# Moving the key products, the decay and a 64x64 block inverse of a chunked gated delta rule beside the input projection

## What is computed

```
gc = cumsum(gdec); decay = where(i >= j, exp(gc_i - gc_j), 0)
A  = I + strict_lower((k*beta) @ k.T * decay);  T = inverse(A)
u = T @ (v*beta);  w = T @ (k*beta*exp(gc));  qk = (q @ k.T) * decay
v_new = u - w @ S;  o = (q @ S)*exp(g) + qk @ v_new
S = S*exp(g_last) + k_dec.T @ v_new            # the only chain from chunk to chunk
```

## Time and profile before

| what | value |
|---|---|
| median of 3 runs | 2875.92 us (2875.68 to 2878.38) |
| profiled execution | 2880.71 us, its span 2878.8 us |
| TensorE busy | 2641.6 us, 92% of the span |
| VectorE, ScalarE, GpSimd busy | 1296.5, 712.8, 444.4 us |
| mean granted clock of TensorE | 0.958 of full speed |
| HBM traffic | 144.32 MB read, 49.27 MB written |

### The profile page before, as it was taken

One profiled execution on the slowest core, in us unless ns is written; L12 is line 12 of the kernel. 1 busy time (PEld: TensorE's weight loads), 2 busy tenths in 40 slices (PEclk: granted clock), 3 DMA queues, 4 the chain that ended last, 5 costly groups with the idle time before them and its releaser, 6 DMA issues.

```text
span 2878.8 us, 39434 instructions
## 1 busy us (share of the span) xinstructions
PE 2641.6 (92%) x14704; PEld 2379.2 (83%) x14704; DVE 1296.5 (45%) x2190; ACT 712.8 (25%) x1269; POOL 444.4 (15%) x1039
## 2 busy tenths in 40 slices
PE   5999999974799999766999999999789999999997
PEld 4999999954788888635889899898678888888886
DVE  5444400003655555354444544445454444444445
ACT  5232211113233333104122121221422121222212
POOL 4000000004566665111000000000420000000002
PEclk9999999986899999877999999999889999999999
DMA  4122222124334333215111011111221111111111
GB/s 139 54 75 78 66 82 71 59 72 129 87 92 118 109 96 88 63 29 172 45 44 58 29 58 44 44 58 31 80 81 45 44 44 44 44 44 44 44 36 66
DMA packets 200686, 194.74 MB, mean 68 GB/s; under 512 B 27147, under 2 KB 172235, under 8 KB 197514
## 3 DMA queue, kind: packets, MB, share of 16 engines
q1 hardware_dynamic: 200594, 193.53, 22.2%
HBM read 144.32 MB, written 49.27 MB: 67 GB/s over the span
## 4 chain that ended last, share of the span: by engine, by line
PE 50%; POOL 2%; issue 1%; ACT 0%; DMA 0%; DVE 0%; SPq 0%; DVEq 0%; POOLq 0%; ACTq 0%
PE bank L124 17%; PE bank L126 17%; PE bank L125 17%; ACT f_relu L142 0%; DMA f_up_raw<-in_w_up_dram 0%; POOL f_acc L1586 0%; PE bank L179 0%; POOL f_acc L1584 0%; POOL fn_rs L113 0%; POOL fn_ms L147 0%; POOL ff_rs L113 0%; POOL ff_rt L111 0%; POOL ff_rt L110 0%; POOL fn_rt L111 0%; POOL fn_rt L110 0%
## 5 line engine op out<-in xcount | busy, mean ns | idle before, releaser
L124 PE MATMUL bank<-f_h_hi,f_up_lo 128*128 128x344 f32 (+1 forms) x1536 | 493.9, 322 | 4.5 <-DVE f_up_lo L1688 2.4
L1693 DVE TENSOR_TENSOR f_acc<-bank,f_acc 128x512 f32<-128x512 f32 x512 | 353.2, 691 | 320.5 <-PE bank L126 320.1
L126 PE MATMUL bank<-f_h_hi,f_up_hi 128*128 128x344 f32 (+1 forms) x1536 | 492.3, 321 | 0.0
L125 PE MATMUL bank<-f_h_lo,f_up_hi 128*128 128x344 f32 (+1 forms) x1536 | 492.1, 320 | 0.0
L124 PE MATMUL bank<-f_dn_hi,f_z_lo 128*128 128x512 f32 x1088 | 432.8, 398 | 0.5 <-ACT f_relu L1621 0.5
L126 PE MATMUL bank<-f_dn_hi,f_z_hi 128*128 128x512 f32 x1088 | 429.6, 395 | 0.0
L125 PE MATMUL bank<-f_dn_lo,f_z_hi 128*128 128x512 f32 x1088 | 428.4, 394 | 0.0
L124 PE MATMUL bank<-h_hi,w_lo 128*128 128x412 f32 (+3 forms) x1000 | 351.7, 352 | 2.1 <-DVE w_lo L427 2.1
L125 PE MATMUL bank<-h_lo,w_hi 128*128 128x412 f32 (+3 forms) x1000 | 351.1, 351 | 0.0
L126 PE MATMUL bank<-h_hi,w_hi 128*128 128x412 f32 (+3 forms) x1000 | 350.9, 351 | 0.0
L124 PEld LDWEIGHTS bank<-f_h_hi,f_up_lo 128*128 128x128 f32 x1536 | 290.9, 189 | 7.9 <-DVE f_up_lo L1688 2.7
(11 more groups left out here) (342 smaller groups left out, 3229.0 us busy)
## 6 DMA issues: line engine op xcount, KB each, us to landing
f_up_raw<-in_w_up_dram SPq DMA_DIRECT2D x64, 512.0 KB, 4.8
f_dn_raw<-in_w_down_dram SPq DMA_DIRECT2D x64, 512.0 KB, 3.7
p_dram<-y SPq DMA_DIRECT2D x24, 1024.0 KB, 4.6
w_raw<-in_w_in_dram SPq DMA_DIRECT2D x24, 512.0 KB, 5.8
xres<-in_x_prompt_dram SPq DMA_DIRECT2D x16, 512.0 KB, 4.6
x_dram<-x SPq DMA_DIRECT2D x16, 512.0 KB, 3.0
f_acc<-x_dram SPq DMA_DIRECT2D x16, 512.0 KB, 5.0
out_y_prompt_dram<-f_acc SPq DMA_DIRECT2D x16, 512.0 KB, 2.7
```

The lines of the kernel that those rows point to most:

```text
L124: pe.matmul(out, wl, xh, start=start and k == 0, stop=False, skip_group_check=skip)
L125: pe.matmul(out, wh, xl, start=False, stop=False, skip_group_check=skip)
L126: last = pe.matmul(out, wh, xh, start=False, stop=stop and k == n - 1, skip_group_check=skip)
L1693: dve.tensor_tensor(dst, bank, dst, ALU.add).then_inc(s["y_added"], 1)
```

## The change

- **Projection.** The 8 columns of a and b are the first tile, not the last; the tiles are reordered (keys first, then queries, values, gMLP v, gate, u), and the loops are unrolled. `gates` runs beside tiles 1 to 3. A new class `Keys` makes, for every chunk, the key product k k^T (one `by_head` on TensorE), the decay (`decay` on GpSimd, `exp` on ScalarE) and on VectorE the norm of the keys and the scaled matrix N, stored in `n_dram`; one chunk per tile at tiles 6 to 12, two at tiles 13 to 16, the last at tile 17. At tile 17 the 64x64 diagonal blocks of all chunks and heads (2 x 4 x 16 = 128 of them, one on each partition) are loaded back in 8 DMAs with runs of 256 bytes, VectorE inverts them by elimination during tiles 18 to 24 (62 steps of two dependent operations on up to 961 elements per partition), and the inverses are stored in `t_dram` at the end of the stage.
- **Mixer.** Key product, decay of N, GpSimd's 16x16 inversion, its DRAM round trip, the masks and two of the three doubling levels are gone. The level from 64 to 128 is left (`x_ready`, `y_ready`), and moved into the pass that loads the chunk. There are 18 passes with three stages (f = n, q = n - 1, o = n - 2). The sums of squares are made by ScalarE with `accum_out`, one for each head, in place of products with ones and a reduction; one `dve_rsqrt` per pass serves both norms. w_o's product is cut in 4 parts. `oT_hi`, `oT_lo`, `xres` and `x1` have two buffers. `build_u` makes the turned inverse in 6 small transposes.

```
+TILES = [None] + [*range(4, 8), *range(0, 4), *range(8, 12), *range(20, 24), *range(12, 16), *range(16, 20)]
+KEYS_AT = {**{6 + n: [n] for n in range(7)}, **{13 + n: [7 + 2 * n, 8 + 2 * n] for n in range(4)}, 17: [15]}
...
+    def load_blocks(self, sp):
+        sp.wait_ge(self.s["n_stored0"], 8 * NCH)
+        sp.wait_ge(self.s["n_stored1"], 8 * NCH)
+        for b in range(2):
+            for h in range(H):
...
+                sp.dma_start(self.blk[rows, :, :], src).then_inc(self.s["blk_loaded"], 16)
...
+    def scale(self, dve, n):
...
+        dve.tensor_tensor(heads(nm), heads(bank[:, :]), across(c.ident[:]), ALU.mult).then_inc(s["diag_made"], 1)
...
+        dve.tensor_reduce(self.ss[:], heads(nm), AX.X, ALU.add).then_inc(s["ss_made"], 1)
...
+        dve_rsqrt(dve, s["rsqrt"], n * DVE_RSQRT_STEPS, rk, self.ms[:], self.rt[:])
...
+        for h in range(H):
+            ins = dve.scalar_tensor_tensor(out=head(nm, h), in0=head(bank, h), scalar=c.negb[:, n, h:h + 1],
+                                           in1=head(self.em[n % 2], h), op0=ALU.mult, op1=ALU.mult)
...
+    def eliminate(self, dve, j):
...
+        rows, cols = HALF - 1 - j, j
+        col = blk[:, j + 1:HALF, j:j + 1].to_broadcast([P, rows, cols])
+        row = blk[:, j:j + 1, 0:j].to_broadcast([P, rows, cols])
...
+        self.own.did(dve, dve.tensor_tensor(part, col, row, ALU.mult))
+        self.own.did(dve, dve.tensor_tensor(below, below, part, ALU.add))
```

```
+            dve.wait_ge(s["vb_squared"], f + 1)
+            dve.tensor_scalar(ms[:, H:H + 1], ss8[:], 1.0 / HW, EPS, ALU.mult, ALU.add).then_inc(s["ms_made"], 1)
...
+            dve_rsqrt(dve, s["rsqrt"], n * DVE_RSQRT_STEPS, rs[:], ms[:], rt[:])
...
+            dve.tensor_tensor(heads(oa[:]), heads(bO), along(rs[:, 0:H]), ALU.mult).then_inc(s["oa_part"], 1)
...
+            dve.scalar_tensor_tensor(out=vbn[:], in0=bF, scalar=rs[:, H:H + 1], in1=c.v_gain[:],
+                                     op0=ALU.mult, op1=ALU.mult).then_inc(s["vbn_made"], 1)
...
+            dve.tensor_tensor(heads(av[:]), heads(vt[:]), along(c.alpha[:, f, :]), ALU.mult).then_inc(s["av_made"], 1)
...
+            dve.tensor_scalar(epsq[f % 2][:], ssq[:], EPS, DK * EPS, ALU.add, ALU.mult).then_inc(s["epsq_made"], 1)
...
+            dve.tensor_tensor(oT_lo[q % 2][:, H:KT, :], heads(ob[:]), oT_hi[q % 2][:, H:KT, :].bitcast(F32),
+                              ALU.subtract).then_inc(s["oTb_lo"], 1)
...
+            dve.tensor_tensor(qkm[:], bE, emQ[:], ALU.mult).then_inc(s["qkm_made"], 1)
```

and in ScalarE's order, after `o_ready`, come the four squares of the output, then, after `pt_k`, the four scaled copies `kd`, then the square of `vb`, the four squares of q and the copy `xs`:

```
+            for h in range(H):
+                ins = act.activation(head(sqo, h), head(bO, h), ACT.Square, accum_out=oss[:, h:h + 1])
...
+            act.activation(junk[:], bF, ACT.Square, accum_out=ss8[:]).then_inc(s["vb_squared"], 1)
...
+                ins = act.activation(head(junk_q, h), head(bD, h), ACT.Square, accum_out=ssq[:, h:h + 1])
...
+            act.activation(xs[:], bY[0:HALF, 0:H * HALF], ACT.Copy).then_inc(s["xs_made"], 1)
```

More of the change, by code:

```diff
@@ L551, in softplus_gates, with kind_of, steps_at, gates @@
     return act, dve, g_made
-def gates(c, io, st):
-    nc, sem, psum = c.nc, c.sem, c.psum
+NB5 = 5
+WB = 412
+HALF = P // 2
+NEVER = 1000.0
+TILES = [None] + [*range(4, 8), *range(0, 4), *range(8, 12), *range(20, 24), *range(12, 16), *range(16, 20)]
+NT = len(TILES)
+KEYS_AT = {**{6 + n: [n] for n in range(7)}, **{13 + n: [7 + 2 * n, 8 + 2 * n] for n in range(4)}, 17: [15]}
+LAST_KEYS = 17
+def kind_of(t):
+    f = TILES[t]
+    return "ab" if f is None else "conv" if f < NCONV else "gate" if f < NCONV + H else "plain"
+def steps_at():
+    total = sum((HALF - 1 - j) * j for j in range(1, HALF - 1))
+    tiles = range(LAST_KEYS + 1, NT)
+    out, done, j = {t: [] for t in tiles}, 0, 1
+    for n, t in enumerate(tiles):
+        while j < HALF - 1 and (done < total * (n + 1) / len(tiles) or t == NT - 1):
+            out[t].append(j)
+            done += (HALF - 1 - j) * j
+            j += 1
+    return out
+STEPS_AT = steps_at()
+def gates(c, io, st, bank, const_made):
+    nc, sem = c.nc, c.sem
     al = st.sb("al_b", [P, H])
@@ new lines, in pe @@
+    def pe(eng, step):
+        if step == 1:
+            for t in range(NCH):
+                last = eng.transpose(bank[0][:, t * 8:(t + 1) * 8], c.ab[:, t * P:(t + 1) * P], c.ident[0:8, 0:8])
+            last.then_inc(ab_turned, 1)
+        elif step == 2:
+            eng.wait_ge(g_made, 1)
+            eng.wait_ge(const_made, CONST_MADE)
+            eng.matmul(bank[1][:, 0:NCH * H], c.upto[:], flat, start=True, stop=True).then_inc(sums, 1)
+            eng.matmul(bank[1][:, NCH * H:2 * NCH * H], c.ones[:], flat, start=True, stop=True).then_inc(sums, 1)
+        else:
+            eng.wait_ge(sums_copied, 1)
+            eng.transpose(bank[0][0:NCH * H, P:2 * P], flat, c.ident[:]).then_inc(g_turned, 1)
@@ new lines, in mix @@
+    ssq, ss8, oss = sb("mx_ssq", [P, H]), sb("mx_ss8", [P, 1]), sb("mx_oss", [P, H])
+    ms, rt, rs = (sb("mx_" + n, [P, H + 1]) for n in ("ms", "rt", "rs"))
+    epsq = two("mx_epsq", (P, H))
+    xres, x1 = two("xres", (P, D)), two("x1", (P, D))
+    wo_raw = (x1[1][:], xres[1][:])
+    oT_hi, oT_lo = two("oT_hi", (P, KT, P), F32R), two("oT_lo", (P, KT, P), F32R)
+    S, ga = c.S, c.ga
+    names = """kt_loaded qt_loaded v_loaded gate_loaded vb_loaded ut_loaded gb_loaded t64_loaded n21_loaded xres_loaded0 xres_loaded1
+        x1_stored0 x1_stored1 delta_stored         zeroed
+        pt_v pt_g pt_b pt_q pt_k qk_ready x_ready y_ready p_ready gm_ready w_ready o_ready sd_ready oT_ready wo_ready
+        x1_made oTa_lo oTb_lo ob_sum u_turned u_final r_made ms_made rsqrt epsq_made vbn_made av_made
+        qkm_made oa_part s_updated
+        xs_made oTa_hi oTb_hi eg_made v_copied g_copied q_squared vb_squared kd_made e_made w_made o_squared
+        oa_made dif_made sel_made ob_made qe_made gg_made""".split()
@@ new lines, in x1_add, with build_u @@
+        wait(dve, s[f"x1_stored{o % 2}"], 16 * (o // 2))
+        dve.tensor_tensor(x1[o % 2][:, cols], (bG, bH)[half], xres[o % 2][:, cols], ALU.add).then_inc(s["x1_made"], 1)
+    def build_u(dve, f):
+        t = heads(T64[f % 2][:])
+        u = heads(U[:])
+        q32 = HALF // 2
+        for b in range(2):
+            for a in range(2):
+                at = b * HALF + a * q32
+                dve.transpose(u[at:at + q32, :, at:at + q32], t[at:at + q32, :, a * q32:(a + 1) * q32])
+            low, up = b * HALF + q32, b * HALF
+            ins = dve.transpose(u[up:up + q32, :, low:low + q32], t[low:low + q32, :, 0:q32])
+        ins.then_inc(s["u_turned"], 1)
@@ L1091, in sp_pass @@
-        if i is not None:
-            sp.wait_ge(s["n_stored"], 16 * (i + 1))
-            wait(sp, s["tb_made"], i)
-            for h in range(H):
-                diagonal = io["n_dram"][i].rearrange("(b r) -> b r", b=BD)[:, 0:SB * HW]
-                blocks = diagonal.rearrange("b (i f) -> b i f", f=HW)[:, :, h * P:h * P + SB]
-                sp.dma_start(blkN[h * BD:(h + 1) * BD, :, :], blocks).then_inc(s["blk_loaded"], 16)
-        if f is not None and f + 1 < NCH:
-            load_raw(sp, f + 1)
@@ L1114, in sp_pass @@
+        if n + 1 < NCH:
+            load_raw(sp, n + 1)
         if n < 2:
```

1133 lines of the change are left out of this document (524 added, 609 removed).

## The result

The changed kernel takes 2797.36 us (median of 4 runs, 2787.67 to 2799.49) where the kernel before takes 2875.8 us: a ratio of 0.9725, 95% interval 0.9696 to 0.9754. That is 78 us less. Run again later beside two of the experiments it took 2797.29 us (ratio 0.9732, 0.9715 to 0.9749). The prediction said 2780, 96 us less, with a range of 2745 to 2815: the direction and the range were right, the gain was 17 us too large.

A forecast was written before the change was run, and what follows sets the result against it. Steady mixer passes were taken as bound by TensorE's work plus its wait for oTb_lo: mixer 30 us later, pass 2 at 718.5, 14 passes of 25.9, sample stage at 1118.8 not 1214.7; 96 less, 2780 us, range 2745 to 2815.

The forecast's parts named there:

- the chain: Mixer's steady pass: pt_b, square, root, then VectorE operations to oTb_lo, which TensorE awaits; a pass of 25.9 us.
- GpSimd's hold: End of a mixer pass: GpSimd's oa and dif slow VectorE's av and oTb_lo, adding 1.4 us.
- The elimination: Projection, tiles 18 to 24: VectorE's inversion of the diagonal blocks takes 111 us, at 0.16 us + 1.04 ns an element.
- the fourth rival: Projection: strided operand makes elimination elements cost 2.3 ns or more, 216 us or more in all; 2875 to 2900, chance 0.04.
- exposed stores: Projection's end: last y and the inverses, 3 MB, go out with nothing to hide them; 12 us against 1.3.
- TensorE's own pass: Mixer's steady pass: TensorE's work sums to 21.8 us, 22.3 corrected, if nothing waits.
- The half clock: Mixer: a 2.8 us stall halves TensorE's clock about half the time, 1.8 us each; 0.9 a pass taken.
- the blocks are there 20 to 27 us into tile 18: Projection: block load of 8 to 14.6 us plus 2 to land makes TensorE wait once, before tile 20; 1.5 us taken.
- The third rival: Projection: block load and elimination 25 to 40% dearer, plus a longer stall at tile 20; 2792 to 2815, chance 0.10.
- the forecast with 0.58: Main case: mixer passes of 24.9 to 26.9 us, total 2766 to 2794, chance 0.58.
- The mixer's first turn: Mixer's start: chunk 0's loads delay the constants, so the first pass begins 15.2 us in, at 674.8.
- the ring of two: Mixer's start: w_o's pieces come through two buffers, holding pass 2 back to 718.5 us.

The follow-up runs named there:

- e3: Changed kernel with VectorE making oTb_lo right after the first of the two sums, not at the end of the pass: 2732.69 us, ratio 0.9489.
- e12: Changed kernel with GpSimd's oa held back until oTb_lo is made, VectorE's order kept: 2750.23 us, ratio 0.9566.
- e13: Changed kernel with ScalarE squaring vb ahead of the four scaled copies kd: 2766.07 us, ratio 0.9623.
- e5: Changed kernel with elimination steps spread over tiles 19 to 24, so VectorE makes tile 20's w_lo before the first step: 2779.02 us, ratio 0.9666.
- e9: Changed kernel with diagonal blocks also stored as long rows, read back in one transfer to 128 partitions: 2780.9 us, ratio 0.9674.
- e6: Changed kernel with w_o's pieces in a ring of four buffers, not two, and chunk 0's xres loaded one pass later: 2786.89 us, ratio 0.9692.
- e2: Changed kernel with SP issuing the load of tile 20's weights ahead of the block load: 2795.34 us, ratio 0.9712.

## Why the prediction was right, and where it was off

**Right, and shown.** The pass came out as walked. Its period was put at 25.9 us and is 25.85; the chain was named link by link, and each of three cuts in it (e3 behind all of it, e12 at GpSimd's hold, e13 at its ScalarE end) shortened the wait by what the rows said. GpSimd's hold was put at 1.4 us, and e12 gives 1.47. But the operations that it fell on were others: `av` and `epsq`, where the prediction named `av` and `oTb_lo`, which took its plain 0.68 us. That the sum came out is in part luck. The elimination was put at 111 us from the price 0.16 us + 1.04 ns an element, and the whole took 111. Its product reads the strided column; its largest operation (992 elements, not the 961 of the section on the change) and its last step are

```profile
583.63 1.19 DVE L482 TENSOR_TENSOR ab<-room 128x992 f32<-128x992 f32 x1
650.49 0.22 DVE L482 TENSOR_TENSOR ab<-room 128x62 f32<-128x62 f32 x1
```

and both fit that price (1.19 and 0.22), so the 2.3 ns an element of the fourth rival are not there. An extra cost of the column's step shows in one place only: the first step has as many elements as the last, but uses each element of the column, 256 bytes from the next, once, and took 0.27 us (527.16 above). In the second step each is used twice, and its 122 elements took 0.29 us, the plain price.

The 12 us of exposed stores were 10.6.

**Right by two errors that cancel.** TensorE's own pass was put at 22.3, with a correction of 2% on a sum of 21.8; it is 21.5 (e3). The half clock was put at 0.9 a pass, as half of the stalls at 1.8 us each; it falls in ten of the 12 passes 3 to 14, and adds 1.6 us on the mean (25.8 less 24.2). The second error is the larger lesson: the two rows at hand (full clock after 2.05, half after 2.68) bracketed the stall, and I split the odds; the stall was 0.05 us from the bad one.

**Wrong: the step "the blocks are there 20 to 27 us into tile 18 ... a stall of 0 to 3 us, I take 1.5".** The stall was 14.4 us. The term that was mis-sized is the load's duration. It was priced at 8 to 14.6 us, and 2 to land, from the rate of the earlier trace rows, whose transfers go to 128 partitions in runs of 512 bytes; the code of the change shows eight transfers to 16 partitions in runs of 256, and it took 23.9 to 29.5. In the changed kernel's trace the blocks then came 39 us into tile 18, which began at 488.0. The rest of the step was right: the share of 19.1 us (18.6 predicted), w_lo behind it, once only. That is 12.9 us over the 1.5 taken, and TensorE then ran at half speed to about 551, some 1.7 us more: the 13.5 us by which the last projection matmul came late, less 1 us by which the other terms were too high. e5 and e9, whose edits lie there alone, give 18 and 16 us back. The third rival had this place ("a longer stall at tile 20") with a price of 12 to 35 us and 0.10 of the chance; its second half, a dearer elimination, did not happen. The measured 2797 lies in that rival's 2792 to 2815, and outside the 2766 to 2794 of the forecast with 0.58: the stated range held because it had been drawn wide enough to take in most of the projection's price.

**Off by a little.** The mixer's first turn came 17.6 us after its start, not 15.2: the last of the constants, issued at 680.82, landed at 687. Passes 0 and 1 took 45.0 (43.7 predicted), set by the ring of two as said: e6 moves their end by 7.3 us.

**The spread.** The changed kernel's runs lie between 2787.7 and 2799.5. The block load varies from 23.9 to 29.5 us between traces and TensorE's wait from 8.5 to 14.4 with it; the time at which tile 17 ends by nearly 3 us. The totals alone don't tie the spread to the load: four runs of the changed kernel spread over 12 us and, run again, over 6.5, of e2, with the same narrow load, over 2.6, and of e9, with the wide one, over 5. What makes the load vary was not looked for.

## What to carry to other kernels

Price a transfer by a row with the same partitions per transfer and the same run length, not by the stage's best rate; where none exists, the bound has to reach well beyond the nearest one. An operation whose inputs have long been ready does not belong behind a dependent chain when the next stage's first instruction waits for it: one moved instruction was worth 65 us, and one changed number in e5, which lets urgent work go ahead of filler that depends on a late transfer, 18. A wait of TensorE of 1.1 or 1.2 us cost its length here and no more; one of 2.05 us cost the clock too in two of 12 passes, one of 2.63 in ten, and so cutting 0.6 us of it (e13) returned 30 us from pass 2 on (370.9 us to the sample stage in place of 401.3).

## What the runs showed of the hardware that was not expected

- 2 MB from DRAM to SBUF: 8.5 us to 128 partitions in one transfer, 19.1 us in eight transfers of 16 partitions, 23.9 to 29.5 us when cut into runs of 256 bytes as well. The share of the DMA engines reads 1.4 in the last case: a high share says that they are occupied, not that they move much.
- Two passes with the same 2.63 us of wait and the same work took 24.2 and 27.0 us, by the granted clock alone (1.00 and 0.88).
- VectorE's `epsq`, four columns and one input in SBUF, took 1.00 us beside GpSimd's `dif` and 0.16 without it.
- A VectorE product of 62 elements took 0.27 us where it steps 256 bytes in its column for every element, and 0.22 where it doesn't step; with a step for every second element the price was the plain one (122 elements, 0.29 us).
